# Second mixer: the decay exponents of a head as two matrix products of 128 rows, sums of squares of three groups on GpSimd, and one tile moved in the order

## The reference, cut to what matters

```python
dt = jax.nn.softplus(dt_raw + dt_bias)
a = -jnp.exp(a_log).reshape(G, R)
cs = jnp.cumsum(dt_c * a, axis=2)                      # along the 128 positions of a chunk
seg = cs[:, :, :, None] - cs[:, :, None, :]
decay = jnp.exp(jnp.where(causal, seg, -jnp.inf))      # 128 x 128 for each chunk and head
cb = jnp.einsum('bclgn,bcsgn->bclsg', c_c, b_c)
y_diag = jnp.einsum('bclsgr,bcsgrp->bclgrp', cb[..., None] * decay, x_dt)
y_off = jnp.einsum('bclgn,bcgrpn,bclgr->bclgrp', c_c, prev, jnp.exp(cs))
y = (y_diag + y_off) + xs * d_skip
y = y * jax.nn.silu(z)
y = _rmsnorm(y.reshape(bsz, s, G, D_INNER // G), 1.0).reshape(bsz, s, D_INNER) * norm_w
```

## Time and profile before

| | |
|---|---|
| median of 3 runs | 1800.03 us |
| the runs | 1799.48, 1805.16, 1800.03 us |
| the profiled execution, its own time | 1806.84 us |
| its span in the profile | 1804.7 us |
| mean granted TensorE clock | 0.998 of full |
| PE, DVE, ACT, POOL busy | 97%, 65%, 63%, 68% of the span |
| second mixer, first tile to last norm | about 391 to 655 us of the span |

### The profile page before, as it was taken

How to read it: one execution, slowest core, us unless ns; L and a number is a source line. 1 busy time by engine, 2 the same in 40 slices (tenths; PEclk the granted TensorE clock), 3 DMA queues, 4 the chain that set the end, 5 groups by cost and what they waited for, 6 DMA issues and landing times.

```text
span 1804.7 us, 24784 instructions
## 1 busy us (share of the span) xinstructions
PE 1752.1 (97%) x8529; PEld 1094.1 (61%) x8688; DVE 1172.4 (65%) x1884; ACT 1129.9 (63%) x1582; POOL 1221.7 (68%) x1776
## 2 busy tenths in 40 slices
PE   7989999998999999999999999999999999999999
PEld 3546666655565556666666666666657776566665
DVE  6886777238888855777127857775257877577720
ACT  8887666455977667666464977665443544866641
POOL 7746777875455557777875657777864454587785
PEclk9999999999999999999999999999999999999999
DMA  7323444443233225444443024444542232244443
GB/s 266 105 94 129 151 141 146 160 153 118 72 94 94 94 80 176 145 148 141 161 131 105 25 71 140 141 152 142 162 115 80 80 94 71 93 153 151 141 159 121
DMA packets 64636, 225.38 MB, mean 125 GB/s; under 512 B 7808, under 2 KB 8192, under 8 KB 64128
## 3 DMA queue, kind: packets, MB, share of 16 engines
q1 hardware_dynamic: 63936, 221.79, 37.9%
q10 hardware_dynamic: 576, 2.01, 0.3%
HBM read 221.57 MB, written 2.10 MB: 124 GB/s over the span
## 4 chain that ended last, share of the span: by engine, by line
PE 77%; DVE 11%; ACT 6%; issue 5%; POOL 1%; DMA 1%; SPq 1%; DVEq 0%; ACTq 0%; POOLq 0%
PE psum L295 22%; PE psum L305 21%; PE psum L337 12%; PE psum L341 11%; PE psum L1785 3%; DVE psum L1593 1%; PE psum L2161 1%; ACT w_big L250 1%; ACT psum L1462 1%; PE psum L2196 1%; DVE psum L1678 1%; PE psum L2178 1%; ACT L1495 1%; DVE arena L1581 1%; POOL w_rest L266 1%
## 5 line engine op out<-in xcount | busy, mean ns | idle before, releaser
L266 POOL TENSOR_TENSOR w_rest<-w_panel,w_big 128x256 bf16<-128x256 f32 x1660 | 1170.6, 744 | 533.8 <-ACT w_big L250 533.8
L295 PE MATMUL psum<-x_big,w_big 128*128 128x512 f32 x2248 | 658.4, 426 | 9.9 <-ACT x_big L387 7.2
L305 PE MATMUL psum<-x_rest,w_rest 128*128 128x512 bf16 x2139 | 538.9, 381 | 7.9 <-DVE x_rest L483 1.7
L250 ACT ACTIVATE w_big<-w_panel 128x1024 fp32r<-128x1024 f32 (+1 forms) x415 | 418.2, 1032 | 172.9 <-PE psum L341 91.0
L295 PEld LDWEIGHTS psum<-x_big,w_big 128*128 128x128 f32 x2248 | 418.3, 189 | 134.1 <-issue 25.4
L305 PEld LDWEIGHTS psum<-x_rest,w_rest 128*128 128x128 bf16 x2248 | 188.6, 98 | 283.4 <-issue 105.1
L701 DVE SCALAR_TENSOR_TENSOR psum<-ffn_raw,params,psum 128x512 f32<-128x512 f32 x352 | 264.5, 751 | 7.2 <-ACT psum L655 1.0
L693 DVE TENSOR_TENSOR ffn_raw<-psum,rstd 128x512 f32<-128x512 f32 x176 | 121.3, 691 | 141.3 <-PE psum L305 120.4
L655 ACT ACTIVATE psum<-ffn_raw,params 128x512 f32<-128x512 f32 x176 | 137.4, 782 | 101.9 <-DVE ffn_raw L693 101.7
L337 PE MATMUL psum<-g_big,w_big 128*128 128x512 f32 x704 | 199.3, 423 | 0.0
L547 DVE SCALAR_TENSOR_TENSOR x_resid<-psum,x_resid 128x512 f32<-128x512 f32 x64 | 43.8, 688 | 225.0 <-PE psum L341 202.2
(11 more groups left out here) (261 smaller groups left out, 1810.2 us busy)
## 6 DMA issues: line engine op xcount, KB each, us to landing
w_panel<-in_up SPq DMA_DIRECT2D x176, 512.0 KB, 3.3
w_panel<-in_dn SPq DMA_DIRECT2D x64, 448.0 KB, 3.1
w_panel<-in_ssd_in SPq DMA_DIRECT2D x41, 512.0 KB, 3.6
w_panel<-in_dn SPq DMA_DIRECT2D x32, 512.0 KB, 3.3
w_panel<-in_hgrn_in SPq DMA_DIRECT2D x32, 512.0 KB, 3.6
w_panel<-in_lru_in SPq DMA_DIRECT2D x18, 512.0 KB, 3.3
w_panel<-in_ssd_out SPq DMA_DIRECT2D x16, 512.0 KB, 3.6
w_panel<-in_swa_in SPq DMA_DIRECT2D x12, 512.0 KB, 3.6
```

The lines of the kernel that those rows point to most:

```text
L250: act.activation(k.w1[:, slot, 0:words], k.w[:, slot, 0:words], ACT.Copy, scale=(SHIFT - 1) / SHIFT).then_inc(k.s("panel_big"), 1)
L266: rest = pool.tensor_tensor(k.w2[:, slot, a], k.w[:, slot, a], k.w1[:, slot, a].bitcast(F32), ALU.subtract)
L295: pe.matmul(out, k.w1[:, slot, q * m:(q + 1) * m], k.x1[:, q, :], start=q == 0, stop=False)
L305: mm = pe.matmul(out, k.w2[:, slot, q * m:(q + 1) * m], k.x2[:, q, :], start=False, stop=q == DT - 1)
```

## The change

**Seg in two products.** The rows of the first product are now all 128: 24 rows with the three parts of the 8 heads of one group (along the row), 12 rows with the three parts of the four chunks' sums (down the rows, with a minus in the moving operand), and 92 rows that add minus 1e30 for blocks of later positions. With 92 rows for 128 positions, 35 places are left out, the even positions up to 68; a second product of 4 x 35 columns with identity-like tables (`odd_left`, `odd_right`) writes them into every other column of the bank. `ncs3`, the identity, the mask and ACT's L1447 go. The weights of all heads (`left`) lie in the arena; the moving operands `right` and `pairs` lie in tiles of `y_rest` that are free until the group's norm.

**Heads in another order.** The rows of dt are laid out as 8 x 4 instead of 4 x 8, and DVE's per-head factors are read with a stride of four.

**DMAs.** Six DMAs on ACT's queue instead of two. In `ssd_sync` there are 15 instead of 12: per part four into `right`, each 8 partitions x 4 groups x 128, and one into `left`, 4 partitions x 32 x 128. SP now waits for the constants first.

**Sums of squares.** For the groups 0 to 2 they go to POOL (`ssd_gpsimd`); for group 3 they stay on DVE.

**Order of tiles.** In the groups 1 to 3 the first z tile (kind 6) comes after x tile 4 and not before it.

```diff
-SSD_ROWS = 3 * SSD_DT
+SSD_ROWS = 3 * SSD_R
+SSD_BLOCK0 = SSD_ROWS + 3 * NC
+SSD_BLOCKS = P - SSD_BLOCK0
+SSD_DOUBLE = P - 1 - SSD_BLOCKS
-SSD_KINDS = [[6, 7, 0, 1, 2, 3, 4, 5, 8, 9]] + [[0, 1, 2, 3, 6, 4, 5, 7, 8, 9]] * (SSD_G - 1)
+SSD_KINDS = [[6, 7, 0, 1, 2, 3, 4, 5, 8, 9]] + [[0, 1, 2, 3, 4, 6, 5, 7, 8, 9]] * (SSD_G - 1)
...
-        pick = b.pick(g, r)
-        bank = 6 - r % 2
-        pe.matmul(k.ps[:, bank, :], pick, b.cs3[0:SSD_ROWS, :], start=True, stop=False)
-        for c in range(NC):
-            pe.matmul(k.ps[:, bank, chunk[c]], b.ncs3[0:SSD_ROWS, chunk[c]], pick, start=False, stop=False)
-        mm = pe.matmul(k.ps[:, bank, :], b.ident, b.mask.unsqueeze(1).to_broadcast([P, NC, P]), start=False, stop=True)
-        mm.then_inc(k.s("ssd_seg"), 1)
+        bank = k.ps[:, 6 - r % 2, :]
+        pe.matmul(bank, b.head(g, r), b.right[:, g, :], start=True, stop=False)
+        even = bank.rearrange("p (c l) -> p c l", l=P)[:, :, 0:2 * SSD_DOUBLE:2]
+        pe.matmul(even, b.odd_left, b.odd_right, start=False, stop=True).then_inc(k.s("ssd_seg"), 1)
...
+    sp.wait_ge(k.s("mixer_landed"), 96)
     for part, ready in enumerate((3, 5, 6)):
         sp.wait_ge(k.s("ssd_chain"), ready)
         for c in range(NC):
-            rows = slice(SSD_DT * c, SSD_DT * (c + 1))
-            sp.dma_start(b.cs3[SSD_DT * part:SSD_DT * (part + 1), c * P:(c + 1) * P], b.parts[part][rows]
+            sp.dma_start(right[SSD_R * part:SSD_R * (part + 1), c], b.parts[part][SSD_DT * c:SSD_DT * (c + 1)]
                          ).then_inc(k.s("ssd_cs_landed"), 16)
+        rows = slice(SSD_ROWS + NC * part, SSD_ROWS + NC * (part + 1))
+        sp.dma_start(b.left[rows], b.parts[part]).then_inc(k.s("ssd_cs_landed"), 16)
...
+    for rows in (slice(0, SSD_ROWS), slice(SSD_BLOCK0, P)):
+        act.dma_start(b.left_words[rows], k.dram["ssd_tables"][rows, 0:SSD_LEFT]).then_inc(k.s("mixer_landed"), 16)
+    for rows, lo, to in ((slice(SSD_ROWS, P), 0, b.right), (slice(0, SSD_ROWS), S // 2, b.pairs)):
+        words = k.dram["ssd_tables"][rows, SSD_LEFT + lo:SSD_LEFT + lo + S // 2]
+        act.dma_start(to[rows].bitcast(F32), words.unsqueeze(1).to_broadcast([words.shape[0], SSD_G, S // 2])
+                      ).then_inc(k.s("mixer_landed"), 16)
-
-    def cs(_, n):
-        act.wait_ge(k.s("ssd_cs_landed"), 16 * 3 * NC)
-        act.activation(b.ncs3[0:SSD_ROWS], b.cs3[0:SSD_ROWS], ACT.Copy, scale=-1.0).then_inc(k.s("ssd_ncs"), 1)
...
+def ssd_gpsimd(pool, k, panel):
+
+    g, t = divmod(panel - 4 - SSD_TURN[0] - 3, 10)
+    if not (0 <= g < SSD_G - 1 and t < SSD_TG):
+        return
+    n = SSD_TG * g + t
+    pool.wait_ge(k.s("ssd_sq"), n + 1)
+    if n:
+        pool.wait_ge(k.s("ssd_sqsum"), n)
+    if t == 0:
+        if g:
+            pool.wait_ge(k.s("ssd_norm_sum"), g)
+        pool.tensor_copy(k.sqsum[:, :], k.sq[:, n % 2, :]).then_inc(k.s("ssd_sqsum"), 1)
+    else:
+        pool.tensor_tensor(k.sqsum[:, :], k.sqsum[:, :], k.sq[:, n % 2, :], ALU.add).then_inc(k.s("ssd_sqsum"), 1)
...
     def sum_(g, t):
+        if g < SSD_G - 1:
+            return
```

## The result

| | before | changed |
|---|---|---|
| median | 1799.77 us | 1808.79 us |
| lowest to highest | 1799.27 to 1805.16 | 1808.29 to 1809.34 (5 runs) |
| span of the profiled execution | 1804.7 | 1807.0 |

The medians are 9.0 us apart. The ratio is 1.004, 95% interval 1.0025 to 1.0055: slower, clear of the noise. (It is reckoned over all executions and not from the medians, whose ratio is 1.005; so one long execution of the kernel before weighs in it.) 1799.6 had been forecast, with a range up to 1807.5.

What follows compares the result with a forecast made beforehand. Head events were taken as paced by ACT and DVE as much as PE. Groups -1.7, last group -0.8 and SP's DMAs +2.1 gave -0.4 us: 1806.4 profiled, carried over to 1799.6; range 1792.5 to 1807.5.

Steps and rivals of the forecast that it cites:

- Constants ... 4 us of cover: Front of the second mixer: constants land at 401.7, SP needs them at 405.7, so nothing waits.
- rival C: Front of the mixer: 92-row constants DMA on few engines lands 0.9 to 4.4 us late; 1800.5 to 1804.0; chance 0.27.
- the stall of 4 us stays: PE's wait at L1599: POOL's run and L1599 move together, so the 3.99 us wait remains.
- rival B: L1599's wait vanishes if POOL's run breaks before DVE arrives: 4.0 us saved, 1795.6; chance 0.08.
- Seg: PE's product of exponents: 0.34 us a head instead of 0.65, 9.9 us less for 32 heads, not all on the path.
- Rival A: PE is the limit throughout: all 9.9 us come back, less 2.1 for DMAs; 1792; chance 0.15.
- Sums and order: Groups with tiles: sums on POOL and the new tile order together make each 0.57 us shorter, 1.7 for three.
- POOL's cover of 0.4: End of a group: POOL's 1.2 us sum ends at 540.3, before PE wants it at 540.71.
- The last group: Group without tiles: PE's 0.2 us lead per event can be gained, 0.8 us over four events.
- SP's block: Front of the mixer: three more DMAs at 0.70 us each cost PE 2.1 us; block about 10.5 us.
- Rival D: SP's new DMA shapes cost 1.40 us each throughout: block 21 us, +10 us, 1810; chance 0.08.
- L1599 under 1 us: DVE's 128x128 product after SP's block: forecast over 4 us again; under 1 us would show the forecast wrong.

Runs made afterwards that it cites:

- right128: Changed kernel with only the 104-row DMA of the right constants made 128 rows, the 24- and 92-row DMAs kept; 1808.61 us, ratio 1.0045.
- left64: Changed kernel with only the left constants' DMAs of 24 and 92 rows made two of 64 rows; 1802.1 us, ratio 1.001.
- before_psum: Kernel before, with the exponentials that L1599 reads written to PSUM instead of SBUF; 1800.03 us, ratio 0.9986.
- e3: Not a run: a head event within a group of heads; the new order gives it a convolution tile instead of the z tile; 4.84 us before, 6.87 after.
- e2: Not a run: the head event just ahead of e3 in a group of heads; 7.70 us from evict to evict before, 6.87 after.
- spread_oldorder: Changed kernel with constants in DMAs of 64, 64 and 128 rows and the tile order of before; 1797.05 us, ratio 0.9982.
- spread: Changed kernel with its constants in DMAs of 64, 64 and 128 rows instead of 24, 92 and 104; 1800.35 us, ratio 0.9998.

## Why the prediction was wrong, point by point

**The step that failed: "Constants ... 4 us of cover".** It took the rate of a 1,024 KB table of 128 rows for 1,635 KB in other shapes. The constants landed at about 413.1 and not at 401.7. This was rival C, on the side of its 0.27. Its place and its first cause were right, as right128 and left64 show; its size was not. It had 0.9 to 4.4 us of lateness, the runs showed 7.4 (413.1 less 405.7). Put into C's own sum, 0.5 + 2.1 + 7.4 gives PE a wait of 10.0, and the trace has 9.95; with 2.3 for the clock the forecast of 1799.6 becomes 1809.3, and 1808.79 was measured. C reckoned one large DMA alone on few engines; the trace has that DMA beside three panels, which took 9.1 us to land and not 3.6. At the 99 GB/s of 408 to 412 the 736 KB alone would need about 7.6 us (an estimate from that row) where C had 16.1, and the DMA took 19 from its issue at about 394; so C came as near as it did with a rate that was too slow and without the sharing. How the landing splits between the few engines and this sharing was not measured apart. The Trainium skill (DMA: Bandwidth & Descriptors, "Why a DMA increments its semaphore by 16 and not by 1") lets a DMA run on the largest number up to 16 that divides its rows: 4 for 92, 13 for 104, 16 for 64 and 128. By that rule left64 should mend most of it and right128 next to nothing, and the runs agree (6.7 us and 0.2), as does the share of 0.25 at the end of the landing.

**The carry-over from one execution.** The sum was made against a profiled execution of 1806.84 that had a stall of 3.99 and a slow clock of 3.4, and its distance to the median was carried along as if it were constant. By before_psum the executions near 1800 do not hold such a stall. So the sentence "the stall of 4 us stays" could only hold for a few executions, and in the profile of the changed kernel it did not hold either. This did not make the forecast of the median wrong, since the -0.4 counts nothing for the stall. It is why the profiles mislead: between them a longer wait and slow clock at 421 (9.4 and 2.3) replace the stall and its clock (7.4), and 3.3 come off in the groups, so their spans are only 2.3 us apart (1804.7, 1807.0), where the medians are 9.0 apart. And it is why rival B's 4.0 us could not be had in the median.

**The ladder.** In medians, against the kernel before at 1799.86: sums on POOL -4.0 (1795.83); the new seg with its 15 DMAs and well-shaped constants +1.2 (1797.05); the new order +3.3 (1800.35); the shape of the constants' DMAs +8.4 (1808.79).

**Seg.** Right: it is 0.30 on PE for a forecast of 0.34 (the second product 0.08, not 0.13), and it isn't on the path. With the sums on DVE it gives nothing, 58.38 for 58.37; with them on POOL 0.5 of its 2.8 a group. Rival A is refuted.

**Sums and order.** The rhythm was right (6.93 forecast, 6.87 measured; e3 lengthened by the order). The group was mis-sized: 1.0 shorter, forecast 0.57. The two edits inside it were netted. Taken apart, the prediction's own terms give the sums 2.0 (0.50, 0.77 and the 0.72 of idle time) and charge the order 1.4 (6.93 less 4.84, less the 0.67 of taps that go). By the runs the sums with the new seg give 2.0 (58.36 to 56.40), and the order costs 1.0: it is the order that was priced too dear.

**POOL's cover of 0.4.** Wrong by sign. The sum takes 1.28 us (forecast 1.2), but its square ended at 543.49 and PE was ready at 544.27, so PE waits 0.63 in each of three groups. The forecast held PE's time for the norm fixed at that of before, 540.71, while the same change made PE earlier, by 0.9 counted from the evict of e2. And even before, PE had waited 0.27 for the sum there. By the rule of the Trainium skill (GPSIMD Engine Reference, 4.1 Engine selection) the prediction's estimate was 1.4; the trace decides for 1.28. The same add on DVE has a median of 0.81 in the trace of before (L1669), so here POOL takes 1.6 times as long.

**The last group.** 0.8 forecast, 0.4 measured (first seg to norm, 23.79 before and 23.39 now). PE's lead of 0.2 an event was used up: L1369 now waits 0.2 for DVE's product with cb.

**SP's block.** 10.8 for 10.5: 0.72 for each of 15 DMAs, 0.70 forecast. Rival D is refuted. In spread_oldorder, where it isn't late, PE's wait is 2.5 for 2.6.

**L1599 under 1 us.** Listed as the sign of rival B. The sign came, and by B's own condition: POOL's run broke into 4 and 12 pieces, and its end at 441.07 lies ahead of the product. The gain did not come, since PE had already stood 9.9 us for the panel and the median had not held the stall.

**What stays open.** PE's wait and the half clock at the front cost 9.9 and 2.3 us in the trace of after, and 5.0 and up to 1.7 in that of `spread`; that is 5.5 of the 6.5 us between these two spans (1807.0, 1800.5). The other microsecond has no row that I can name. For the medians the same rows give 8.5 of the 9.0: 9.95 and 2.3, less the 0.4 that PE waits there in an execution of 1800.01 (before_psum), less 2.9 for three groups and 0.4 for the last.

## What to carry to other kernels

Give each DMA of constants a row count that spreads (64 or 128 and not 92), even if it then loads rows that are overwritten; and when a queue is made to wait for something new, work out the landing time with everything else that is in flight. Read what a stall is worth in the execution that the median stands for: a stall that only some executions have can neither be saved nor hide a new wait. Where engines keep one rhythm, price each edit by what it does to the pacing engine: 12 sums taken from DVE were worth 4 us, 11 us of matrix work taken from PE 2.5.

## What the runs showed of the hardware that I had not expected

- One DMA of 92 rows and 736 KB, issued at about 394, landed at about 413; for the last 6 us the DMA share was that of four engines of 16. The panels beside it took 9.1 us to land (3.6 before). Not all of that is due to the 92 rows: with the constants in 64 and 128 rows they took 6.8 (`spread`) and 4.9 (spread_oldorder), in single profiles.
- After PE had stood still for 9.95 us the clock was at the 1.2 GHz level for 10.2 us; after waits of 2.46, 3.88 and 5.01 us (spread_oldorder, left64, `spread`) for about 3.4 us each; after the 3.99 of before for 6.8. The length of the wait does not set it alone.
- A 128x128 product on DVE with both inputs in SBUF took 0.28 us with POOL idle (441.27, changed kernel), 0.34 to 0.56 within POOL's run of 16 pieces, and 4.67 or 4.68 within the same run in other executions; with one input in PSUM it took 0.28. The Trainium skill (GPSIMD Engine Reference, 1. Specifications) has GpSimd and VectorE share SBUF's interface where a VectorE instruction has two inputs in SBUF; before_psum agrees, and no run here shows why it is so seldom long.
